# Eight modulation chunks leave three turnings of a two-block transformer kernel, and unit products take their places

## The reference

```python
for l in range(DEPTH):
    mx = jnp.split((jax.nn.silu(c) @ w_mod[l] + b_mod[l])[:, None, :], N_MOD, axis=-1)
    mz = jnp.split(jax.nn.silu(c_ctx) @ w_mod[l] + b_mod[l], N_MOD, axis=-1)
    x = x + 0.5 * mx[2] * swiglu(modulate(rms_norm(x), mx[0], mx[1]), ffn1_w1[l], ffn1_w3[l], ffn1_w2[l])
    z = z + 0.5 * mz[2] * swiglu(modulate(rms_norm(z), mz[0], mz[1]), ffn1_w1[l], ffn1_w3[l], ffn1_w2[l])
    hx = modulate(rms_norm(x), mx[3], mx[4]) @ w_in[l]
    hz = modulate(rms_norm(z), mz[3], mz[4]) @ w_in[l]
    mix_x, mix_z = token_mixing(hx, hz, ...)          # Fourier, neighbourhood, gated linear, grouped attention
    x = x + mx[5] * (mix_x @ w_out[l])
    x = x + 0.5 * mx[8] * swiglu(modulate(rms_norm(x), mx[6], mx[7]), ffn2_w1[l], ffn2_w3[l], ffn2_w2[l])
    # z gets the same two steps in the first layer only
```

## Time and profile before

| | us |
|---|---|
| median of 3 runs | 3241.92 (3236.0 to 3253.08) |
| profiled execution, its own time | 3237.68 |
| its span, first to last instruction | 3235.9 |
| TensorE busy in it | 3118.6 (96%) |
| mean granted TensorE clock | 0.987 of 2.4 GHz |

### The profile page before, as it was taken

The page is one execution under the profiler, slowest core; times in us unless marked ns, Lnnn a source line. Parts: engine busy times, 40 slices in busy tenths (PEclk is TensorE's granted clock), DMA queues, the critical chain, the costliest instruction groups (busy, mean ns, idle before and its releaser), DMA issues.

```text
span 3235.9 us, 55079 instructions
## 1 busy us (share of the span) xinstructions
PE 3118.6 (96%) x23504; PEld 2828.6 (87%) x23504; DVE 1764.9 (55%) x2769; ACT 1507.0 (47%) x2294; POOL 147.8 (5%) x143
## 2 busy tenths in 40 slices
PE   7999999999999999999999999999999999999998
PEld 5899788897879998989898879999899899989987
DVE  3446454564436554445555445455766556576655
ACT  3344445453445444345443444446654444665443
POOL 0000100001000000000200000000010101101000
PEclk9999999999999999999999999999999999999999
DMA  7865445763535555765355345555445564435553
GB/s 254 272 202 181 137 141 168 228 194 116 152 130 192 175 184 195 251 220 178 125 164 174 124 144 183 182 161 154 124 151 187 176 203 150 139 110 162 174 195 130
DMA packets 465135, 556.73 MB, mean 172 GB/s; under 512 B 25420, under 2 KB 431868, under 8 KB 464508
## 3 DMA queue, kind: packets, MB, share of 16 engines
q1 hardware_dynamic: 464892, 553.21, 53.1%
HBM read 552.12 MB, written 1.05 MB: 171 GB/s over the span
## 4 chain that ended last, share of the span: by engine, by line
PE 82%; DVE 9%; ACT 3%; DMA 3%; issue 2%; SPq 0%; POOL 0%; DVEq 0%; ACTq 0%
PE psum L121 23%; PE psum L123 22%; PE psum L122 22%; DVE wl L2179 2%; PE psum L728 1%; DVE wl L278 1%; PE psum L1534 1%; DMA wr<-in_ffn_w_dram 1%; PE psum L2344 1%; PE psum L129 1%; PE psum L2450 1%; PE psum L2428 1%; PE psum L1209 1%; PE psum L1890 1%; PE psum L1521 1%
## 5 line engine op out<-in xcount | busy, mean ns | idle before, releaser
L278 DVE TENSOR_TENSOR wl<-wr,wh 128x1024 fp32r<-128x1024 f32 (+1 forms) x558 | 656.6, 1212 | 243.5 <-ACT wh L267 242.2
L267 ACT ACTIVATE wh<-wr 128x1024 fp32r<-128x1024 f32 (+1 forms) x558 | 555.6, 1039 | 167.0 <-DMA wr<-in_ffn_w_dram 147.2
L121 PE MATMUL psum<-xt_hi,wh 128*128 128x256 f32 (+1 forms) x2000 | 569.4, 285 | 7.0 <-DVE wl L2179 4.8
L122 PE MATMUL psum<-xt_lo,wh 128*128 128x256 f32 (+1 forms) x2000 | 558.9, 279 | 0.0
L123 PE MATMUL psum<-xt_hi,wl 128*128 128x256 f32 (+1 forms) x2000 | 558.9, 279 | 0.0
L2179 DVE TENSOR_TENSOR wl<-wr,wh 128x1024 fp32r<-128x1024 f32 (+3 forms) x336 | 389.7, 1200 | 78.4 <-ACT wh L2171 77.1
L121 PEld LDWEIGHTS psum<-xt_hi,wh 128*128 128x128 f32 (+1 forms) x2000 | 374.9, 187 | 19.7 <-DVE wl L2179 8.4
L122 PEld LDWEIGHTS psum<-xt_lo,wh 128*128 128x128 f32 (+1 forms) x2000 | 374.4, 187 | 1.9
L123 PEld LDWEIGHTS psum<-xt_hi,wl 128*128 128x128 f32 (+1 forms) x2000 | 375.0, 188 | 0.1
L121 PE MATMUL psum<-wh,xt_hi 128*128 128x256 f32 (+1 forms) x1280 | 368.1, 288 | 1.9 <-ACT vv L3311 1.9
L2171 ACT ACTIVATE wh<-wr 128x1024 fp32r<-128x1024 f32 (+3 forms) x336 | 322.7, 997 | 97.7 <-DMA wr<-in_mlp_w_dram 71.6
(11 more groups left out here) (491 smaller groups left out, 5547.6 us busy)
## 6 DMA issues: line engine op xcount, KB each, us to landing
wr<-in_ffn_w_dram SPq DMA_DIRECT2D x231, 1024.0 KB, 5.4
wr<-in_w_in_dram SPq DMA_DIRECT2D x88, 1024.0 KB, 5.3
wr<-in_w_mod_dram SPq DMA_DIRECT2D x72, 1024.0 KB, 5.1
wr<-in_mlp_w_dram SPq DMA_DIRECT2D x64, 1024.0 KB, 5.2
wr<-in_w_out_dram SPq DMA_DIRECT2D x20, 1024.0 KB, 5.0
wr<-in_mem_w_kv_dram SPq DMA_DIRECT2D x8, 1024.0 KB, 5.0
wr<-in_w_branch_dram SPq DMA_DIRECT2D x16, 512.0 KB, 3.4
wr<-in_w_branch_dram SPq DMA_DIRECT2D x8, 1024.0 KB, 4.9
```

What stands on the lines that cost most here:

```text
L121: pe.matmul(out, a[0], b[0], start=first, stop=False)
L122: pe.matmul(out, a[0], b[1], start=False, stop=False)
L267: act.activation(self.high[s][:, r], self.raw[s][:, r], ACT.Copy).then_inc(self.highs.sem, 1)
L278: dve.tensor_tensor(self.low[s][:, r], self.raw[s][:, r], self.high[s][:, r].bitcast(F32), ALU.subtract).then_inc(self.lows.sem, 1)
```

## The change

The list of pieces changes in three places, and the unit products with it. M1[12:16] go from turning A into `xf2`, behind its pieces 5, 11, 17 and 23. M1[24:26] go from turning B into `zf3`. M1[34:36] go from turning C to the end of the pieces that carry the wide attention; their `steps` stay at two. The unit products inside the removed pieces go, and 24, 16 and 16 of them are put ahead of the diag products of A, B and C (step 1 of the stage).

```diff
-    order += xf2.pieces
+    order += weave(xf2.pieces, M1[12:16], 5, 6)
...
-    order += M1[12:16]
...
-    order += zf3.pieces[0:3] + x_in1.pieces + zf3.pieces[3:]
+    order += zf3.pieces[0:3] + x_in1.pieces + weave(zf3.pieces[3:], M1[24:26], 16, 4)
...
-    order += M1[24:26]
...
-    order += M1[26:34]
+    order += M1[26:36]
...
-    order += M1[34:36]
...
-    for p_, n in ((zf1.up1[0], 5), ..., (xf3.up1[0], 2), (M1[35], 3)):
+    for p_, n in ((zf1.up1[0], 5), ..., (xf3.up1[0], 2)):
         p_.cover = n
-    for p_, n in ((M1[13], 4), (M1[15], 3), (M1[25], 3), (M1[35], 5)):
-        p_.cover_turn = n
     z_t0.cover = {1: 4}
-    x_t7.cover, z_t9.cover = {1: 2}, {1: 3}
+    x_t7.cover, z_t9.cover, x_t9.cover = {1: 24}, {1: 16}, {1: 16}
```

More of the change, by code:

```diff
@@ L4047, in first_block @@
     w.queue(order)
-    for p_, n in ((zf1.up1[0], 5), (zf1.down[4], 4), (xf2.up1[2], 4), (x_out1.pieces[0], 5), (zk.gate, 10), (xf3.up1[0], 2), (M1[35], 3)):
+    for p_, n in ((zf1.up1[0], 5), (zf1.down[4], 4), (xf2.up1[2], 4), (x_out1.pieces[0], 5), (zk.gate, 10), (xf3.up1[0], 2)):
         p_.cover = n
-    for p_, n in ((M1[13], 4), (M1[15], 3), (M1[25], 3), (M1[35], 5)):
-        p_.cover_turn = n
     z_t0.cover = {1: 4}
-    x_t7.cover, z_t9.cover = {1: 2}, {1: 3}
+    x_t7.cover, z_t9.cover, x_t9.cover = {1: 24}, {1: 16}, {1: 16}
     zm.fourier.cover, xm1.fourier.cover = {2: 9}, {2: 7}
```

## The result

| | before | after |
|---|---|---|
| median, 19 executions each | 3236.09 | 3253.18 |
| lowest to highest | 3228.69 to 3254.35 | 3244.12 to 3292.31 |
| profiled execution, its own time | 3237.68 | 3252.42 |
| its span | 3235.9 | 3250.6 |
| mean granted TensorE clock | 0.987 | 0.983 |

The ratio is 1.0067, with a 95% interval of 1.005 to 1.0084. The change makes the kernel slower, by a little over the half per cent that I had set as the border of "same". The median lies in my range, but I had forecast 6 us more and it is 17. Seven of the 19 executions after are at 3260 to 3292; none before is above 3255.

A forecast was written before the change was run, and what follows sets the result against it. TensorE, busy 96% of the span, was taken to bound the kernel. Terms -3.4 + 2.1 + 8.8 - 1.3 gave +6.2 us: 3243.9 on the profiled execution's scale, 3248 on the median's, range 3236 to 3262.

The forecast's parts named there:

- turning A: From last xf2 product to first xf3 product: 20.2 us becomes 10.5, four chunks cost 6.3 in xf2; net -3.4 us.
- turning B: From zf3 to the gate piece of zk, 13.0 us: two chunks add 2.6 in zf3, 0.5 gained; +2.1 us.
- turning C: From x_out1 to xf4, 14.7 us plus 1.2 of waits: becomes 14.6 with 4.3 idle, low clock; -1.3 us.
- The bound with the clock lost: Upper case for turning B: 2.0 idle us cost the clock, 14.5 us against 12.5, so +4.1.
- Entry: Entry to x_out1 (5.0 us): two more chunks, late load, 3.7 us idle, low clock; +8.8 us, bounds 6.9 to 8.8.
- The ring: Four load slots, ahead of x_out1: first w_out chunk asked for only when M1[32] is used, 1906.9, split from 1912.7.
- Rivals 1 and 2: Before x_out1 and in turning C: first, clock holds, +2.4 us, chance 0.22; second, ring doesn't bind, -0.8, chance 0.10.
- The sum: Whole kernel: -3.4 + 2.1 + 8.8 - 1.3 = +6.2 us, with bounds together +1.2 to +10.7.
- rival 3: At the turnings and entry: unit products don't hold the clock, 5.0 us per stretch, +15.7 on +6.2, 3264; chance 0.08.

The follow-up runs named there:

- the kernel with the exit: Changed kernel with 22 and 14 unit products ahead of the wide attention, plus 14 more behind its first modulation chunk: 3249.67, ratio 1.0029.
- the filled kernel: Changed kernel with 22 and 14 unit products, not 18 and 9, in the two key turns ahead of the wide attention: 3263.95, ratio 1.0047.
- the entry alone: Kernel before with only M1[34:36] moved behind M1[33] and 16 unit products in turning C: 3247.11, ratio 1.0036.
- a plain shift: Kernel before with 16 unit products ahead of one up piece in the middle of zf3: 3241.28, ratio 0.998.
- A alone: Kernel before with only M1[12:16] moved into xf2 and 24 unit products in turning A: 3234.71, ratio 0.9996.
- holes covered: Changed kernel with 22 unit products ahead of M1[35]'s turns and 34 instead of 16 in turning C: 3246.47, ratio 1.0007.
- candidate: Kernel before with M1[12:16] in xf2, M1[34:36] in xf4, 24 unit products in turning A and 34 in turning C: 3237.74, ratio 1.0015.

## Why the prediction was right, and where it was not

- **Turning A: right.** Diag products after 5.8 us (5.7 measured), no DMA in the chain, 10.5 with waits (9.7, and 0.7 that `xf3`'s first products lose to waits for `xt_lo`). The chunks in `xf2` were put at 6.3; the ten profiles with them have 5.5 to 8.1 over before, in the one of after a wait of 1.4 us for `wl` at 1135 that was 0.9 is part of it. Sum -3.4 forecast, -2.1 in the profile of after.
- **Turning B: right.** +2.1 forecast; 3.0 in `zf3` (2.6 forecast) and -0.4 in the turning, +2.5. The bound with the clock lost was 14.5; 13.8 to 14.0 was seen in three profiles.
- **Entry: mechanism right, size low.** The ring, the split ahead of M1[35]'s rows, the hole released by L750 and the low level behind it all came. The hole was 3.7 in one profile, as forecast, and 5.1 in the one of after, since the chunk landed later. With `x_out1` at 23.1 to 24.1 in place of 22.1, the two stages together are 9.4 to 11.2 us longer in the six profiles without the cover (10.4 in the one of after), where 8.8 was the forecast and the upper bound. Rivals 1 and 2 fell by this.
- **C: right.** The hole of 4.1 us, the low level in it, and -1.4: -0.7 in the turning, and -0.7 in `xf4`'s first piece, where the waits for `xt_lo` are shorter. -1.3 was the forecast.
- **The sum: 6.2 forecast, 9.4 by the stages of the first profile, 8.6 by the medians of the kernel with the exit.** The mechanisms were right; 1.6 of the 3.2 us are the entry, 1.3 are A. The medians moved by 17.1. By my border of half a per cent that is slower, which had 0.11 of the chance, and not "same", which had 0.86. That the median lies in the range of 3236 to 3262 is owed in part to the range's width: its upper part was there for rival 3, which isn't what happened.
- **The step that failed** is the first one: "I work out a difference from the trace and put it on the median." It took the attention's 10 us at 0.50 as a fixed part of every execution. It isn't fixed. The fourteen profiles, all with the same attention (one has 14 unit products more in it), have 0, 3, 10, 38, 41 and 89 us, and the filled kernel alone had 0 in one execution and 38 in another. Seven of 19 executions after are 7 to 39 us above 3253; they raise the mean from 3250.0 (the other twelve) to 3259.5. In the profiles of the filled kernel and of the entry alone such executions have the attention's long stretch; for the changed kernel itself none was profiled in one.
- **Rival 3** saw the right place and drew the wrong reason from it. It took the earlier trace rows as a sign that unit products don't hold the level and priced it at 5 us per turning. The level stayed low among the narrow attention products, and the price is 14 or 36 us. That their narrowness keeps it low is a reading: no run changed their shape. My sentence against it, that these products don't stand in a turning, was true and led me to drop the place.

The Trainium skill, "TensorE: Matmul & The Clock Gate", section "Why this matters for your kernels", advises no idle gap over about 3 us. The runs show that keeping to it isn't enough: the level fell behind 2.2 idle us in the decays, and behind 0.7 in the attention of the filled kernel with the exit (1849.3). Once low, it stayed at 1.2 GHz through 89 us with no idle stretch, and the advice doesn't speak of that.

**What stays open.** Why executions are long more often in some orders: nine of twelve with the holes filled, seven of 19 in the changed kernel, six of 123 before, while a plain shift gave none. What ends a low stretch: the places found are pauses of L1983, but other pauses passed without a return. The counts of the single parts (1 or 2 of 12) can't be told from before. And the twelve shorter executions of after have a mean 13.9 us above before's median, 4.5 above the stage sum, which I can't place.

## What to carry to other kernels

Before a difference is put on a median, look in the profile for a stretch where TensorE is fully busy at half the clock: its length may be a draw, and a second profile of the same kernel tells. A few dense products where a run of half-filled ones pauses are worth a try: with 14 of them the median was 14 us lower and none of twelve executions was long, where nine had been, though on another chip and with no profile that shows them at work. A piece that moves is priced with all that it brings along: the two chunks brought three turns into `xf4`, where one had been counted. And a piece that is moved "into" a carrier stage must be looked up in the order: here it fell behind it, ahead of a stage whose first load takes the ring place that it occupies.

## What the runs showed of the hardware

- Dense products have two paces at a granted clock of 1.00. In the 432 of `x_in1` they start 0.114 us apart before (49.1 us in all) and 0.118 in four other profiles (51.0 us): A alone, holes covered, filled with exit, candidate; `x_out1` takes 22.1 or 22.9 in the same way, with all of it at full clock. What picks the pace wasn't tried.
- Filling a hole with unit products didn't protect the stage behind it: with 0.9 and 1.2 idle us ahead of the attention filled, one profile had no low stretch there and another 37.6 us, and nine executions in twelve were long. Whether the fill made them so isn't shown.
- The same instructions of the attention took 56.3, 60.2, 73.8 and 74.6 us, and 96.7 in one profile, as TensorE stood at 1.2 GHz for 0, 10, 38, 41 and 89 us of them.
